# A hold on GpSimd's split of a stage's third unit, and a last norm with fewer operations

## What is computed

```python
for l in range(DEPTH):            # DEPTH = 2
    mix = token_mixing(x, w_in[l], ..., w_out[l], cos, sin)
    x = layer_norm(DN_ALPHA * x + mix, ln1_g[l], ln1_b[l])
    x = layer_norm(DN_ALPHA * x + swiglu_ffn(x, w_gate_up[l], w_down[l]), ln2_g[l], ln2_b[l])
```

## Time and profile before

| | |
|---|---|
| median of three runs | 2342.47 us |
| the profiled execution | 2347.63 us, span 2345.8 us |
| TensorE matmuls, busy | 2261.1 us, 96% of the span |
| VectorE | 1113.9 us, 47% |
| GpSimd | 1142.9 us, 49% |
| ScalarE | 833.2 us, 36% |
| mean granted TensorE clock | 0.987 |

### The profile page before, as it was taken

The page is one execution under the profiler, slowest core; times in us unless marked ns, Lnnn a source line. Parts: engine busy times, 40 slices in busy tenths (PEclk is TensorE's granted clock), DMA queues, the critical chain, the costliest instruction groups (busy, mean ns, idle before and its releaser), DMA issues.

```text
span 2345.8 us, 34138 instructions
## 1 busy us (share of the span) xinstructions
PE 2261.1 (96%) x13464; PEld 1823.5 (78%) x13464; DVE 1113.9 (47%) x1948; ACT 833.2 (36%) x2220; POOL 1142.9 (49%) x674
## 2 busy tenths in 40 slices
PE   8999999999999899999999999999899999999997
PEld 6777877877777788888777778778677787888885
DVE  4677677764444611110256776777544466111003
ACT  3555445466641211110135454444665403111100
POOL 5453333324337466666544442332343375666664
PEclk9999999999999999999999999999999999999998
DMA  4221111111124223322222211211111332322322
GB/s 152 72 81 48 48 57 57 43 50 46 55 79 143 75 91 98 99 92 97 92 99 72 81 47 41 64 51 51 41 55 55 108 108 90 99 92 97 117 90 81
DMA packets 53886, 182.64 MB, mean 78 GB/s; under 512 B 7520, under 2 KB 8160, under 8 KB 53728
## 3 DMA queue, kind: packets, MB, share of 16 engines
q1 hardware_dynamic: 48976, 167.01, 22.1%
q10 hardware_dynamic: 4752, 13.45, 1.6%
HBM read 169.94 MB, written 4.19 MB: 74 GB/s over the span
## 4 chain that ended last, share of the span: by engine, by line
PE 86%; DVE 9%; issue 2%; ACT 2%; DMA 1%; POOL 0%; DVEq 0%; ACTq 0%; POOLq 0%
PE PS L586 19%; PE PS L588 18%; PE PS L587 18%; PE PS L754 11%; PE PS L844 2%; PE PS L958 2%; PE PS L1025 2%; PE PS L830 2%; PE PS L972 1%; PE PS L848 1%; PE PS L903 1%; PE PS L887 1%; PE PS L781 1%; PE PS L894 1%; PE PS L924 1%
## 5 line engine op out<-in xcount | busy, mean ns | idle before, releaser
L547 POOL TENSOR_SCALAR wh<-w_raw 128x1024 fp32r<-128x1024 f32 (+1 forms) x255 | 277.1, 1087 | 1029.5 <-DMA w_raw<-stream 1028.6
L550 POOL TENSOR_TENSOR wl<-w_raw,wh 128x1024 fp32r<-128x1024 f32 (+1 forms) x255 | 615.5, 2414 | 21.3
L586 PE MATMUL PS<-xh,wh 128*128 128x512 f32 x992 | 398.2, 401 | 11.1 <-issue 6.1
L588 PE MATMUL PS<-xl,wh 128*128 128x512 f32 x992 | 390.3, 393 | 0.0
L587 PE MATMUL PS<-xh,wl 128*128 128x512 f32 x992 | 389.2, 392 | 0.0
L586 PEld LDWEIGHTS PS<-xh,wh 128*128 128x128 f32 x992 | 188.2, 190 | 57.3 <-issue 12.7
L588 PEld LDWEIGHTS PS<-xl,wh 128*128 128x128 f32 x992 | 187.7, 189 | 40.6
L587 PEld LDWEIGHTS PS<-xh,wl 128*128 128x128 f32 x992 | 188.6, 190 | 37.4
L754 PE MATMUL PS<-xh,wh 128*128 128x512 f32 x448 | 205.3, 458 | 5.1 <-DVEq L1692 3.4
L2000 DVE TENSOR_TENSOR hf<-sg,PS 128x512 f32<-128x512 f32 x44 | 30.3, 688 | 355.5 <-PE PS L588 355.5
L1645 DVE SCALAR_TENSOR_TENSOR conv_acc<-PS,cw,conv_acc 128x510 f32<-128x510 f32 x192 | 143.9, 749 | 105.3 <-ACT conv_acc L1187 99.8
(11 more groups left out here) (293 smaller groups left out, 4779.3 us busy)
## 6 DMA issues: line engine op xcount, KB each, us to landing
w_raw<-stream SPq DMA_DIRECT2D x254, 512.0 KB, 3.4
w_raw_spare<-stream SPq DMA_DIRECT2D x46, 512.0 KB, 3.5
x<-x_in ACTq DMA_DIRECT2D x6, 512.0 KB, 7.0
qx<-qx SPq DMA_DIRECT2D x48, 64.0 KB, 2.0
raw<-raw SPq DMA_DIRECT2D x32, 64.0 KB, 2.2
ln_g<-ln_rows ACTq DMA_DIRECT2D x4, 512.0 KB, 4.0
ln_b<-ln_rows ACTq DMA_DIRECT2D x4, 512.0 KB, 5.0
x_park<-x ACTq DMA_DIRECT2D x4, 512.0 KB, 5.0
```

What stands on the lines that cost most here:

```text
L547: nc.gpsimd.tensor_scalar(wh[s][:, w], w_raw[s][:, w], 1.0, 1.0, ALU.mult, ALU.mult).then_inc(w_hi_done, 1)
L550: nc.gpsimd.tensor_tensor(wl[s][:, w], w_raw[s][:, w], wh[s][:, w].bitcast(F32), ALU.subtract).then_inc(split_done, 1)
L586: mm(o, ah, bh, start=first, stop=False)
L588: return mm(o, ah, bl, start=False, stop=last)
```

## The change

**GpSimd.** Ahead of the load's wait for the third unit of a stage behind a norm, GpSimd waits for all eight low parts of that norm. This is at three places: GU of layer 0, the first stage of layer 1, and GU of layer 1. (The first stage of layer 0 is left as it was.) Since GpSimd takes its work in turn, the fourth unit, and in the first stage of layer 1 the split of `ba_raw`, stand behind the wait too.

**Last norm.** Chunk 3 is now ((x - mean) * ln_g) * rs + ln_b in two kinds of SCALAR_TENSOR_TENSOR: one over the whole chunk, and then two halves. ScalarE no longer normalises its half, and VectorE's L1936 and the chunk's factor `ln_nm` are gone. GpSimd does gain and offset of chunk 0 but only the gain of chunk 1; VectorE adds ln_b of chunk 1. SP stores chunk 0, then 2, then 1, then the halves of chunk 3.

```diff
@@ SP, end of the kernel
-            for c in (0, 1):
-                sp.wait_ge(x_affine_pool, c * 2 + 2)
+            sp.wait_ge(x_affine_pool, 2)
+            sp.dma_start(out[:, 0, :], x[:, 0, :]).then_inc(stored, 16)
+            for n, c in ((3, 2), (4, 1)):
+                sp.wait_ge(x_affine, (DEPTH * 2 - 1) * 8 + n)
                 sp.dma_start(out[:, c, :], x[:, c, :]).then_inc(stored, 16)
-            sp.wait_ge(x_affine, (DEPTH * 2 - 1) * 8 + 2)
-            sp.dma_start(out[:, 2, :], x[:, 2, :]).then_inc(stored, 16)
@@ GpSimd, loop over the units u
+                    if u % UNITS == AT_GU * 2 + 2 or u == l * UNITS + 2 > 2:
+                        pool.wait_ge(x_lo, l * 16 + (16 if u % UNITS > 2 else 8))
                     pool.wait_ge(loaded[s], USE[u] * 16)
@@ GpSimd, end of the kernel
-                pool.wait_ge(x_affine_pool, c * 2 + 1)
-                nc.gpsimd.tensor_tensor(x[:, c, :], x[:, c, :], ln_b[:], ALU.add).then_inc(x_affine_pool, 1)
+                if c == 0:
+                    pool.wait_ge(x_affine_pool, 1)
+                    nc.gpsimd.tensor_tensor(x[:, c, :], x[:, c, :], ln_b[:], ALU.add).then_inc(x_affine_pool, 1)
@@ ScalarE, normed
+                        if m == DEPTH * 2 - 1 and c == CHUNKS - 1:
+                            return
@@ VectorE, norm, before factors(3)
+                    if final:
+                        dve.wait_ge(ln_loaded, m * 32 + 32)
+                        STT(x[:, 3, :], x[:, 3, :], ln_mv[:, 3, 0:1], ln_g[:], ALU.subtract, ALU.mult).then_inc(x_affine, 1)
+                        dve.wait_ge(ln_sqrt, m * 4 + 4)
+                        nc.vector.reciprocal(ln_rs[:, 3, :], ln_rs[:, 3, :]).then_inc(ln_factor, 1)
...
+                        dve.wait_ge(x_affine_pool, 3)
+                        TT(x[:, 1, :], x[:, 1, :], ln_b[:], ALU.add).then_inc(x_affine, 1)
+                        dve.wait_ge(ln_factor, m * 8 + 7)
+                        for half in range(2):
+                            w = slice(half * 512, (half + 1) * 512)
+                            STT(x[:, 3, w], x[:, 3, w], ln_rs[:, 3, :], ln_b[:, w], ALU.mult,
+                                ALU.add).then_inc(x_affine, 1)
+                        return
```

More of the change, by code:

```diff
@@ L1934, in norm @@
                     variance(3)
+                    if final:
[3 more added lines that the diff above has]
+                        nc.vector.reciprocal(ln_rs[:, 3, :], ln_rs[:, 3, :]).then_inc(ln_factor, 1)
+                        dve.wait_ge(x_norm, m * 4 + 3)
+                        TT(x[:, 2, :], x[:, 2, :], ln_g[:], ALU.mult).then_inc(x_affine, 1)
+                        dve.wait_ge(x_affine, m * 8 + 2)
+                        TT(x[:, 2, :], x[:, 2, :], ln_b[:], ALU.add).then_inc(x_affine, 1)
+                        dve.wait_ge(x_affine_pool, 3)
[6 more added lines that the diff above has]
+                        return
                     factors(3)
@@ L1937, in norm @@
                        ALU.mult).then_inc(x_norm_tail, 1)
-                    if final:
-                        dve.wait_ge(ln_loaded, m * 32 + 32)
-                        dve.wait_ge(x_norm, m * 4 + 3)
-                        TT(x[:, 2, :], x[:, 2, :], ln_g[:], ALU.mult).then_inc(x_affine, 1)
-                        dve.wait_ge(x_affine, m * 8 + 1)
-                        TT(x[:, 2, :], x[:, 2, :], ln_b[:], ALU.add).then_inc(x_affine, 1)
-                        for half in (1, 0):
-                            w = slice(half * 512, (half + 1) * 512)
-                            if half == 1:
-                                dve.wait_ge(x_norm_tail, m + 1)
-                            else:
-                                dve.wait_ge(x_norm, m * 4 + 4)
-                            TT(x[:, 3, w], x[:, 3, w], ln_g[:, w], ALU.mult).then_inc(x_affine, 1)
-                        for half in range(2):
-                            w = slice(half * 512, (half + 1) * 512)
-                            dve.wait_ge(x_affine, m * 8 + 4 - half)
-                            TT(x[:, 3, w], x[:, 3, w], ln_b[:, w], ALU.add).then_inc(x_affine, 1)
-                        return
                     def scaled(k):
```

## The result

| | before | after |
|---|---|---|
| median of 20 runs each | 2344.53 us (2341.01 to 2348.43) | 2352.79 us (2344.97 to 2358.52) |
| the profiled execution | 2347.63 us, span 2345.8 us | 2355.32 us, span 2353.5 us |
| TensorE matmuls, busy | 2261.1 us | 2260.6 us |
| mean granted TensorE clock | 0.987 | 0.988 |

After to before is 1.0036, with a 95% interval of 1.0027 to 1.0045: the changed kernel is slower by 8.3 us. The forecast was 2343.1 us in a range of 2337.0 to 2348.5, so the measured time lies outside it, where rival 2 put it (2351 to 2354).

The account below looks back on a forecast made before the run. TensorE bounds the chain (86%), with time to win where it stands in the norms. Terms -3.1 + 1.2 + 2.1 - 0.9 = -0.7 us, with 1.4 for the clock +0.7 on the median: 2343.1 us, range 2337 to 2348.5.

Parts of the forecast that it names:

- rival 2: GU stages: GpSimd gets no turn until VectorE's updates are through; unit 2 +5.9 and +6.8 us; 2351 to 2354; chance 0.12.
- The two GU stages: GU, both layers: splits of units 2 to 4 alternate with VectorE's eight updates; loss 1.2 us in layer 0, 2.1 in layer 1.
- I take two updates ahead of GpSimd: GU stages: two updates end at t = 2.2, counted from the new end of the low parts; unit 2 usable at 6.6.
- The low parts' gain: Norms before the held stages: low parts end earlier by 1.65 us (GU layer 0), 1.59 (GU layer 1), 2.03 (first stage).
- rival 1: GU stages: GpSimd's turn comes after one update; unit 2 ready at t = 5.4, unit 4 0.8 us later; 2344.7 us; chance 0.15.
- Nothing more is lost: GU stages behind unit 4: GpSimd (5.33 us or less a unit) keeps up with TensorE (5.5), so no further loss or gain.
- First stage of layer 1: No two-SBUF-input VectorE work there; the `ba` product starts at 1187.6 instead of 1190.68, gain 3.1 us.
- Last norm: End of kernel: VectorE ends 1.8 us earlier, but the stores come together; gain 0.9 us, between 0.5 and 1.8.
- The 1.4 us for the clock: Stretches behind the low parts: a quarter of 5.5 us that only the old kernel gains in executions with a better clock.

## Why the prediction was wrong

**The step that failed** is the one headed "The two GU stages": "I take two updates ahead of GpSimd", for both stages alike. It made one mechanism out of rows that held two. 814.58 and 1980.30, where GpSimd got in only behind the last update, fit the shut-out case; 1918.82 is the case with turns. The kernel with the first stage's hold alone has two more such requests, both made during the seventh update, and both were served only behind the eighth. I read the old rows as "one or two operations slip ahead, then they alternate" and took a compromise, unit 2 ready at t = 6.6, that no stage shows. What happens is either a turn at the first boundary, or none up to the end of the run. Rival 2 named the second of these and gave it 0.12, with the argument that the turns at 1917 stood against it; they don't, since the outcome differs from one meeting to the next.

**Point by point.**
- The low parts' gain was right: none takes over 0.69 us, where one had taken 2.33, and the low parts ended 1.4 to 2.4 us earlier (25.27 and 26.02 against 27.62 and 27.41).
- Layer 0 had turns, by rival 1's order (one update ahead): unit 2 could be used at t = 5.4, as that rival said, and `hf(0)` ended at t = 19.66 (44.93 - 25.27), where rival 1 had 19.7 and the forecast 18.9. Unit 4 was late by 1.3 us (44.99 against 43.70), close to the forecast's 1.2, because the low parts ended 0.7 us earlier than counted. The term was still too small: it stopped at the start of unit 4. Behind the wait of 2.87 us unit 4 took 7.20 us instead of 5.47, another 1.7, and the stretch cost 3.0. "Nothing more is lost" was wrong.
- Layer 1 was shut out: unit 2 at 38.58 instead of 31.67 is +6.9 us, rival 2's +6.8, and the clock behind the stand brought it to +8.7. The forecast had +2.1. This one stage is 6.6 of the 8.4 us between the sum (-0.7) and the pair of profiles (+7.7), and layer 0 is 1.8.
- First stage of layer 1: 3.1 us were forecast, and 2.55 are in the pair of profiles. Over all profiles the small product began 31.36 to 33.57 us behind the norm's start in the four kernels without this hold, 32.5 on the mean, and 30.38 to 31.10 in the seven with it, 30.6 on the mean: the hold is worth about 1.9 us. The term was too large because I took one profile in which TensorE had much of the lower clock ahead of that product (0.78); with the last norm alone and no hold it began at 31.36.
- Last norm: -0.9 forecast, -0.9 between the profiles, with the parts of it as worked out (VectorE's end 1.6 earlier instead of 1.8, 0.75 more between that and the end of the span instead of 0.9).
- The 1.4 us for the clock went to the wrong place. I gave it to executions in which the old kernel has a better clock; what the profiles show is 1.7 to 1.8 us behind each long wait of the new one (1.5 to 3.0 behind the long waits of the other held kernels).

**What the runs make of the total.** With one stage of turns (+3 to +5), one shut out (+8), the first stage -1.9 and the last norm -0.9, the sum is +8 to +10, and +8.3 was measured. The parts measured alone give +14.3, -1.4 and +0.9, in all +13.8; the GU holds' interval alone runs from 11.5 to 17.1, that of the whole change from 6.3 to 10.6, and the other two parts take 0.5 from the first, so they hardly meet; the second measurement of the whole change, 4.7 to 12.0, overlaps with it. Part of the gap is in the profiles: against twice 377.3 the two GU stages lost 13.0 us in the kernel with the GU holds alone (14.3 by its time), and 11.2 and 11.5 in the two profiles of the changed kernel, where the other parts take 2.8 off. A mix of the two outcomes that differs between executions would give the rest, and the wider spread of the changed kernel too (13.6 us over 20 runs, 7.4 before). That is an argument and was not shown: only the profiled executions tell which outcome a stage had, and the two of the changed kernel had the same.

## What to carry to other kernels

When a GpSimd operation is moved, look at what VectorE has queued at its new place: here a run of operations with both inputs in SBUF was either stretched to twice its length or shut GpSimd out to its end, and both have to be priced with the unit that runs at the lower clock behind the wait. Where old rows of one pair of engines show two behaviours, make them two cases with a chance each, and not a compromise between them. The remedy was not to time the request better but to take VectorE's run apart, one operation behind each step of the loop: with all holds and the new last norm that kernel was 5.7 us faster than the one before. Moving the updates alone gave nothing, and the GU holds alone lost 14 us.

## What the runs showed of the hardware

- A GpSimd request that meets a run of VectorE operations with two SBUF inputs (eight of 128x1024, pitch 1.14 us) is either served at the next boundary (high part 1.3 to 1.9 us where it asked early in an operation, alone 1.05) or waits for the whole run (9.5 to 10.1 us). Repetitions of the same piece, but for the width of its first operation, did both, 27 and 5 times. The Trainium skill, SBUF — State Buffer, "Who interferes with whom", says that the port pair that the two share is an exclusive lock and that issue order decides who is blocked. That one of the two stands still at a time agrees with the rows shown here; that issue order decides does not cover the shut-out case, where seven later updates went ahead of a request made during the first.
- Once GpSimd has had one turn, the two alternate, one operation each, as long as GpSimd has splits to make, in every case seen: in the stages a split of a unit takes 5.33 us instead of 3.5, an update 2.05 or 3.4 instead of 1.22.
- TensorE's first unit behind a stand of 2.87 us, and behind one of 8.61 us, took 7.2 us each, against 5.44 to 5.47 at full clock, with the granted clock of those stretches at 0.76 and 0.75. Over all profiles with such a stand it was 7.0 to 8.5 us, and 7.11 and 8.41 behind the same 2.88 us.
